# Delta rule of a hybrid decoder layer: four tiles a batch, instead of one tile at a time with the last one's scan inside

## The reference

```python
kk = jnp.einsum('nbhid,nbhjd->nbhij', kc * bc, kc)
lower = jnp.where(tri_strict, kk * decay, 0.0) + jnp.eye(c)
sol = lax.linalg.triangular_solve(lower, rhs, left_side=True, lower=True, unit_diagonal=True)
attn = jnp.einsum('nbhid,nbhjd->nbhij', qc, kc) * decay
def step(s, xs):
    u0_, wk_, attn_, qd_, kd_, gl_ = xs
    u = u0_ - jnp.einsum('bhid,bhde->bhie', wk_, s)
    o = jnp.einsum('bhid,bhde->bhie', qd_, s) + jnp.einsum('bhij,bhje->bhie', attn_, u)
    s = s * gl_[..., None, None] + jnp.einsum('bhid,bhie->bhde', kd_, u)
    return s, o
...
merged = gate[..., :D_MODEL] * (o_att @ lp['w_att_out']) + gate[..., D_MODEL:] * (o_dn @ lp['w_dn_out'])
```

## Time and profile before

| | us |
|---|---|
| median of 3 runs (lowest, highest) | 1683.84 (1683.21, 1685.87) |
| profiled execution, time | 1685.92 |
| profiled execution, span of the core | 1684.1 |
| PE busy | 1656.2 (98%) |
| weight loads busy (beside PE) | 1601.9 (95%) |
| DVE busy | 969.8 (58%) |
| ACT busy | 587.9 (35%) |
| POOL busy | 526.3 (31%) |

### The profile page before, as it was taken

The page is one execution under the profiler, slowest core; times in us unless marked ns, Lnnn a source line. Parts: engine busy times, 40 slices in busy tenths (PEclk is TensorE's granted clock), DMA queues, the critical chain, the costliest instruction groups (busy, mean ns, idle before and its releaser), DMA issues. The chain is left out here.

```text
span 1684.1 us, 34791 instructions
## 1 busy us (share of the span) xinstructions
PE 1656.2 (98%) x13952; PEld 1601.9 (95%) x13952; DVE 969.8 (58%) x1565; ACT 587.9 (35%) x1190; POOL 526.3 (31%) x287
## 2 busy tenths in 40 slices
PE   8999999999999999999999999999999999999996
PEld 7999999999999888899999999999999999999996
DVE  2001227889466677762853799877777777111157
ACT  3123334444432545542431553222322233201224
POOL 1212111111211112122431424655555554614410
PEclk9999999999999999999999999999999999999998
DMA  4111016445663455426661034444445317431202
GB/s 190 38 50 40 36 37 195 110 122 123 189 212 103 145 158 150 119 90 221 234 235 38 26 139 157 156 156 156 171 168 189 131 75 278 157 117 50 78 8 94
DMA packets 144594, 216.44 MB, mean 129 GB/s; under 512 B 66113, under 2 KB 109409, under 8 KB 142689
## 3 DMA queue, kind: packets, MB, share of 16 engines
q1 hardware_dynamic: 143488, 213.09, 37.7%
q10 hardware_dynamic: 1008, 1.98, 0.4%
HBM read 162.44 MB, written 80.00 MB: 144 GB/s over the span
## 5 line engine op out<-in xcount | busy, mean ns | idle before, releaser
L873 POOL TENSOR_TENSOR wl<-stage,wh 128x1024 fp32r<-128x1024 f32 x81 | 195.7, 2416 | 726.6 <-ACT wh L1565 718.8
L993 PE MATMUL U<-xh,wh 128*128 128x344 f32 x960 | 312.0, 325 | 0.2 <-ACT qkv L1569 0.2
L993 PE MATMUL U<-xl,wh 128*128 128x344 f32 x960 | 307.2, 320 | 0.0
L993 PE MATMUL U<-xh,wl 128*128 128x344 f32 x960 | 307.1, 320 | 0.0
L993 PEld LDWEIGHTS U<-xh,wh 128*128 128x128 f32 x960 | 181.0, 189 | 0.6 <-ACT qkv L1569 0.5
L993 PEld LDWEIGHTS U<-xh,wl 128*128 128x128 f32 x960 | 181.1, 189 | 0.0
L993 PEld LDWEIGHTS U<-xl,wh 128*128 128x128 f32 x960 | 181.0, 188 | 0.0
L1565 ACT ACTIVATE wh<-stage 128x1024 fp32r<-128x1024 f32 x77 | 81.0, 1052 | 131.2 <-PE U L993 108.0
L1104 PE MATMUL U<-xl,wh 128*128 128x344 f32 x384 | 126.3, 329 | 0.0
L1104 PE MATMUL U<-xh,wh 128*128 128x344 f32 x384 | 125.7, 327 | 0.0
L1104 PE MATMUL U<-xh,wl 128*128 128x344 f32 x384 | 125.6, 327 | 0.0
(11 more groups left out here) (456 smaller groups left out, 4441.8 us busy)
## 6 DMA issues: line engine op xcount, KB each, us to landing
stage<-in_wu SPq DMA_DIRECT2D x126, 512.0 KB, 4.3
out_shift<-in_cache SPq DMA_DIRECT2D x16, 1022.0 KB
hid_scr<-cc SPq DMA_DIRECT2D x22, 516.0 KB, 3.0
gate_scr<-gth SPq DMA_DIRECT2D x16, 516.0 KB, 3.5
gates<-gate_scr SPq DMA_DIRECT2D x8, 1032.0 KB, 5.9
dn_scr<-thb SPq DMA_DIRECT2D x12, 512.0 KB, 2.9
tok_scr<-pre SPq DMA_DIRECT2D x48, 128.0 KB, 4.0
qkv<-in_cache SPq DMA_DIRECT2D x10, 512.0 KB, 6.7
```

Of the source, the lines that this page charges most:

```text
L873: nc.gpsimd.tensor_tensor(wl[:, par, :], stage[:, par, :], wh[:, par, :].bitcast(F32), ALU.subtract).then_inc(w_lo, 1)
L993: ins = nc.tensor.matmul(dst, a[:, par, w], b[:, xk, third(j)], start=first and n == 0 and m == 0, stop=last and n == len(ks) - 1 and m == 2)
```

## The change

The tiles go in two batches of four. A batch has three phases.

1. Four fronts, each with eight quarters of gate work behind it (FRONT_FILL). Their products alternate between the banks B34 and B56. LTq, Lo32, Loff, XTq, X, Y, Lb, Xw, XT, ATm, kd, vp and dqk hold four tiles; ET, qkt, dv and Ew still hold one.
2. Six rounds of the inverse over the 16 blocks of four tiles and heads, in two halves of eight: first products of both halves, then second products of both, then the quarters of LEVEL_FILLS. ACT's and DVE's operations take a half each.
3. Four scans in a row, each with four quarters in three places (SCAN_FILLS). The transpose of the last tile's output stands inside.

To make room, oh and ol are no longer written tile by tile, as the batch's tiles lie in their place. The gated outputs (of) and the merged heads (om) go to memory, o_scr, and after the last scan six loads of 512 KB bring them back as of_raw, from which ACT and DVE form oh and ol. 74 quarters of gate work (STATE_FILLS) stand on PE behind the last scan, and 26 with the samples. The heads of the next tile are loaded when this tile's are merged.

```diff
-BESIDE_TILE = (2, 1, 1, 1, 1, 1, 1, 1, 1)
-BESIDE_SAMPLES = GATE_UNITS - EARLY - sum(BESIDE_TILE)
+BATCH = 4
+FRONT_FILL, LEVEL_FILLS, SCAN_FILLS, END_FILL = 8, (1, 1, 1, 1, 3, 2), (1, 1, 2), 2
+LATE_UNITS = GATE_UNITS - EARLY
...
+                LTq, XTq, X, Y, Lo32 = (held(zone, n, [P, BATCH * DN_H, QB]) for n in ("LTq", "XTq", "X", "Y", "Lo32"))
+                Lb = [held(zone, f"Lb{n}", [P, BATCH * DN_H, QB]) for n in range(2)]
+                Xw, Loff, Yw = (held(zone, n, [P, BATCH * DN_H, HB]) for n in ("Xw", "Loff", "Yw"))
+                XT, ATm = (held(zone, n, [P, BATCH, DN_H * P]) for n in ("XT", "ATm"))
...
+            def out_store(t):
+                sp.wait_ge(of_ready, t + 1)
+                sp.dma_start(o_scr[2:6, :, t * P:(t + 1) * P].rearrange("f p t -> p f t"), of[:, t % 2]).then_inc(out_stored.sem, 16)
...
+            for q, ts in batches():
+                for t in ts:
+                    if t + 1 < TILES:
+                        sp.wait_ge(decay_weighted, t + 1)
+                        decays(t + 1)
+                        sp.wait_ge(kd_ready, t + 1)
+                        kq_turned(t + 1)
+                        sp.wait_ge(vp_ready, t + 1)
+                        v_turned(t + 1)
+                    if t == ts[0] and t > 0:
+                        out_store(t - 1)
+                    beside.run(FRONT_FILL + (END_FILL if t == ts[0] and t > 0 else 0))
+                for n in LEVEL_FILLS:
+                    beside.run(n)
+                for t in ts:
+                    if t > ts[0]:
+                        out_store(t - 1)
+                    after(sp, of_ready, t)
+                    sp.dma_start(zin[:], dn_scr[12:16, :, t * P:(t + 1) * P].rearrange("f p t -> p f t")).then_inc(z_in, 16)
+                    if t + BATCH < TILES:
+                        sp.wait_ge(ks_done, 2 * t + 2)
+                        qk_rows(t + BATCH)
+                    sp.wait_ge(ao_ready, t + 1)
+                    sp.dma_start(o_scr[0:2, :, t * P:(t + 1) * P].rearrange("f p t -> p f t"), om[:]).then_inc(merge_stored.sem, 16)
+                    if t + 1 < TILES:
+                        heads_in(t + 1)
+                    beside.run(sum(SCAN_FILLS))
             sp.wait_ge(s_ready, TILES + 1)
             sp.dma_start(O["pS"], S[:]).then_inc(state_stored, 16)
...
+            out_store(TILES - 1)
+            sp.wait_ge(od_done, 2 * TILES)
+            sp.wait_ge(state_stored, 16)
+            since(sp, out_stored, 16 * TILES)
+            since(sp, merge_stored, 16 * TILES)
+            for k in range(6):
+                sp.dma_start(of_raw[:, k, 0:SEQ], o_scr[k]).then_inc(branch_in[k].sem, 16)
...
+            def front(t):
+                key_bank, query_bank = FRONT_BANKS[t % 2]
+                pe.wait_ge(dn_in, 16 * (t + 1))
+                if t == 0:
+                    pe.wait_ge(ao_high, 1)
+                if t % BATCH > 1:
+                    pe.wait_ge(at_ready, t - 1)
+                elif t >= BATCH:
+                    pe.wait_ge(o_ready, t - t % BATCH)
+                k, r = dqk[:, t % BATCH, 4:8, :], dqk[:, t % BATCH, 0:4, :]
+                for h, c in HEADS:
+                    nc.tensor.matmul(key_bank[:, c], k[:, h, :], k[:, h, :], start=True, stop=True)
...
+            def first_products(q, lv, a):
+                bank = FIRST_BANKS[a]
+                if lv == 0:
+                    pe.wait_ge(x_turned, 2 * q + a + 1)
+                    pe.wait_ge(at_ready, (q + 1) * BATCH)
+                else:
+                    pe.wait_ge(x_added, added_of(q, lv - 1, a))
+                if lv == LEVELS - 1:
+                    pe.wait_ge(xt_diag, 2 * q + 1)
+                for m in BLOCKS_OF[a]:
+                    if lv < LEVELS - 2:
+                        for r in QUARTER:
+                            ins = nc.tensor.matmul(bank[r, block_cols(m, QB)], Lb[(lv + 1) % 2][r, m, :], X[r, m, :],
...
+            def second_products(q, lv, a):
+                bank = SECOND_BANKS[a]
+                pe.wait_ge(y_taken, step_of(q, lv, a))
...
+            def scan(t, first):
+                q, b = t // BATCH, t % BATCH
                 pe.wait_ge(s_ready, t + 1)
+                if first:
+                    pe.wait_ge(xt_ready, turned_of(q, LEVELS - 1, 1))
                 else:
+                    pe.wait_ge(o_ready, t)
+                for h, c in HEADS:
+                    ins = nc.tensor.matmul(B34[:, 0, c], dqk[:, b, 4 + h, :], S[:, c], start=True, stop=True)
                 ins.then_inc(ks_done, 1)
+                for h, c in HEADS:
+                    ins = nc.tensor.matmul(B34[:, 1, c], dqk[:, b, h, :], S[:, c], start=True, stop=True)
+                ins.then_inc(ks_done, 1)
+                beside.run(SCAN_FILLS[0])
                 pe.wait_ge(r_ready, t + 1)
+                for h, c in HEADS:
+                    ins = nc.tensor.matmul(B34[:, 0, c], XT[:, b, c], us[:, c], start=True, stop=True)
                 ins.then_inc(u_done, 1)
+                if not first:
+                    turned(t - 1)
+                beside.run(SCAN_FILLS[1])
                 pe.wait_ge(u_taken, t + 1)
+                for h, c in HEADS:
+                    ins = nc.tensor.matmul(B34[:, 0, c], kd[:, b, h, :], us[:, c], start=True, stop=True)
+                ins.then_inc(od_done, 1)
                 pe.wait_ge(qs_taken, t + 1)
+                for h, c in HEADS:
+                    ins = nc.tensor.matmul(B34[:, 1, c], ATm[:, b, c], us[:, c], start=True, stop=True)
                 ins.then_inc(od_done, 1)
+                beside.run(SCAN_FILLS[2])
+
...
+            for q, ts in batches():
+                for t in ts:
+                    front(t)
+                    if t == ts[0] and t > 0:
+                        beside.run(END_FILL)
+                        turned(t - 1)
+                    beside.run(FRONT_FILL)
                 for lv in range(LEVELS):
+                    for a in (0, 1):
+                        first_products(q, lv, a)
+                    for a in (0, 1):
+                        second_products(q, lv, a)
+                    beside.run(LEVEL_FILLS[lv])
+                for t in ts:
+                    scan(t, t == ts[0])
+
+            beside.run(STATE_FILLS[0])
+            turned(TILES - 1)
+            beside.run(STATE_FILLS[1])
+            pe.wait_ge(of_ready, TILES)
...
+            for k in range(6):
+                beside.run(2)
+                since(act, branch_in[k], 16)
+                nc.scalar.activation(oh[:, k, 0:SEQ], of_raw[:, k, 0:SEQ], ACT.Copy).then_inc(of_high, 1)
+            nc.scalar.activation(oh[:, 0:2, SEQ:TOK], osm[:], ACT.Copy).then_inc(of_high, 1)
+            beside.run(STATE_FILLS[1] - 12 - 3)
...
+            def first_blocks(q, a):
+                pr = pair_of(a)
+                dn.link(nc.vector.tensor_tensor(XTq[:, pr], LTq[:, pr], lev(0, 8), ALU.mult))
+                nc.vector.tensor_tensor(XTq[:, pr], XTq[:, pr], fourth(D_IDQ, 8), ALU.add).then_inc(xt_ready, 1)
+                nc.vector.tensor_tensor(Lb[1][:, pr], LTq[:, pr], lev(1, 8), ALU.mult)
...
+            def heads_merged(t):
+                if t > 0:
+                    since(dve, merge_stored, 16 * t)
+                dn.link(nc.vector.tensor_tensor(ot[:, 0], ot[:, 0], ot[:, 1], ALU.add))
+                nc.vector.tensor_tensor(om[:], ot[:, 0], ot[:, 2], ALU.add).then_inc(ao_ready, 1)
...
+            for q, ts in batches():
+                for t in ts:
+                    key_norms(t)
+                    query_norms(t)
+                    if t == ts[0] and t > 0:
+                        out_scaled(t - 1)
+                    masks(t)
+                    if t == ts[0] and t > 0:
+                        out_gated(t - 1)
+                    if t + 1 < ts[0] + BATCH:
+                        decay_rows(t + 1)
+                    if t % 2 == 1:
+                        first_blocks(q, t % BATCH // 2)
+                rounds(q)
+                if ts[0] + BATCH < TILES:
+                    decay_rows(ts[0] + BATCH)
+                for t in ts:
+                    residual(t)
+                    decayed_state(t)
+                    if t > ts[0]:
+                        out_scaled(t - 1)
+                    heads_weighted(t)
+                    new_state(t)
+                    if t > ts[0]:
+                        out_gated(t - 1)
+                    out_norms(t)
+                    heads_merged(t)
+            out_scaled(TILES - 1)
+            out_gated(TILES - 1)
+            for k in range(6):
+                dve.wait_ge(of_high, k + 1)
+                nc.vector.tensor_tensor(ol[:, k, 0:SEQ], of_raw[:, k, 0:SEQ], oh[:, k, 0:SEQ].bitcast(F32), ALU.subtract).then_inc(
+                    of_low, 1)
...```

```

(22 more changed lines are left out.)

580 lines of the change are left out of this document (228 added, 352 removed).

## The result

The changed kernel takes 1764.7 us (median of four runs, 1763.9 to 1765.2) where the kernel before takes 1684.4 beside it (1683.2 to 1685.9): a ratio of 1.048, with a 95% interval of 1.046 to 1.049. It is slower by 80 us, not by the 30 that were forecast, and outside the range of 1688 to 1740.

The account below looks back on a forecast made before the run. PE's instruction stream was taken to bound the kernel (busy 98%). Shorter stream -15, waits at fronts +17.8, scans +13.6, end +10, clock +4 gave +30 us on the median, 1714 us; range 1688 to 1740.

Parts of the forecast that it names:

- I cost the rounds without a wait: Inverse rounds: copy, add and transpose of one half hide beside the other half's 0.76 us burst and the quarter.
- a batch: 25.9: PE time for a batch's six inverse rounds: 15.5 for rounds 0 to 3, 4.2 for round 4, 6.2 for round 5.
- the higher price of a record past the 32nd: Small-product bursts: if half of 2,368 records past the 32nd took twice 12 ns, 14 us more; not assumed.
- if the rounds take 6 us or more each (burst rate or clock): Sign of being wrong, in the inverse rounds: four tiles of a round were forecast at 3.9 us.
- the rounds run at 1.2 GHz: Rival: small products don't restore the clock after the wait, up to 40 us of rounds double, 1745 us; 10%.
- The fronts: Load loop 9.2 us against PE's 6.95 a front; PE waits 7.5 us before the first batch's rounds, 10.3 before the second's.
- the queue ahead of tile 1's loads: First batch's fronts: loads of tile 1 queue behind heads_in(0), 2.4 us.
- the delay of first_blocks: Fronts: first_blocks on DVE, behind the wait for ET, pushes the third tile's Ew 1.4 us further.
- The 13.6 us: Scans: heads' loop of 11.3 us against PE's 8.5 a scan costs 6.8 a batch, 13.6 in all.
- The end: After the last scan: 47.3 us of PE work, plus 10 us of waits for reloaded heads and weights, bounds 2 and 16.
- the 3 us for ACT's late evictions and splits: At the end, ACT waits for reloaded heads: PE loses 1 us, then 2 for weights that ACT splits late.
- the 4.0 put apart for the clock: Slow clock after long PE waits, about 1.5 us each at two fronts and the end, 4 us in all.

Follow-up runs that it names:

- the lump run: Changed kernel with 24 gate quarters moved from the tail into rounds 0 to 3, four together behind each round's last burst: 1754.1 us.
- spread: Changed kernel with 24 gate quarters moved from the tail into rounds 0 to 3, one behind each of a round's four bursts: 1756.8 us.
- the run with late heads: Changed kernel with DVE adding a tile's weighted heads after its new state, gated output and norms, not before the new state: 1752.3 us.
- the 33.5 us: Saving of the changed kernel with rounds 0 to 3's 32x32 products reading fp32 operands' upper halves as bf16, halving their instructions: 1731.2 us.

## Why the prediction was wrong, step by step

- **The rounds: the step that failed.** "I cost the rounds without a wait", with "a batch: 25.9". The price of a record was not the fault: as long as instructions are there, a burst of 64 at full clock takes less than the forecast's 0.76 us (128 in 1.23 with the change behind them). What was left out is the supply: 512 instructions in 7.6 us. Rounds 0 to 3 took 62.2 us instead of 31.0, so 31 us of the 48 by which the profiled span missed. Neither bound had it: the higher price of a record past the 32nd was put at 14 us at most. Its own sign of being wrong, "if the rounds take 6 us or more each (burst rate or clock)", came with 7.6 and 8.0 us, but for neither of the two reasons that it names.
- **The clock in the rounds.** Rounds 4 and 5 took 30.1 us instead of 20.8, 9 us more; at clock 1.00, in the lump run, they take 9.5, better than the 10.4 of the forecast; spread they take 11.9 at 0.86 and 17.0 at 0.59. So the clock is the cause. The rival "the rounds run at 1.2 GHz" had this mechanism at 10%, with 31 us as its price. It was right on the clock and wrong on where it counts: in rounds 0 to 3 the half clock is hidden behind the supply. The Trainium skill (TensorE: Matmul & The Clock Gate, "Part 1: The HAM clock gate") has the slow clock as the default that activity lifts; the 0.50 in the idle wait ahead of round 0 agrees, and the traces add that in the run with 12 quarters a front PE was busy for 12.70 of 12.70 us in rounds 4 and 5, and the granted clock was 0.69 on the mean.
- **The fronts.** Forecast 35.3 (four of 6.95 and 7.5 waited) and 40.0 (with 1.9 of extra work and 10.3 waited), measured 36.8 and 43.3. PE's wait ahead of round 0 was 8.0 us in the first batch (7.5 forecast) and 7.3 in the second (10.3 forecast), where PE also waited 3.8 us for ACT to evict gate work (gth), which the forecast did not have; the loop was 9.3 where 9.2 was worked out. DVE's Ew, tile by tile, as in the earlier trace rows:

```profile
530.15 0.68 DVE L2326 TENSOR_TENSOR Ew<-ET,rn 128x512 f32<-128x512 f32 x1
545.18 0.68 DVE L2326 TENSOR_TENSOR Ew<-ET,rn 128x512 f32<-128x512 f32 x1
554.49 0.69 DVE L2326 TENSOR_TENSOR Ew<-ET,rn 128x512 f32<-128x512 f32 x1
563.86 0.68 DVE L2326 TENSOR_TENSOR Ew<-ET,rn 128x512 f32<-128x512 f32 x1
```

  The first gap is 15.0 instead of 11.6, the second 9.3 instead of 10.6, the third 9.4 instead of 9.2: the queue ahead of tile 1's loads was undersized, and the delay of first_blocks, put at 1.4 for the third tile, didn't come. So part of the fit of the wait is luck. The landings were qkt 5.2 and ET 4.2 us, which the earlier trace rows had at 4.1 and 5.3.
- **The scans.** Forecast 40.3 a batch, measured 44.4 and 39.0 (the second from 747.5 to the first quarter of the tail at 786.5, which is the transpose's 793.6 less its wait of 4.6 and four quarters). DVE waited as forecast, in six scans (its list of waits; us in total, times, longest):

```profile
DVE ot L2415 <- DMA wb<-w_scr: 27.7, 6, 5.7
```

  wb landed in 5.0 us. The 13.6 us were about right: the run with late heads gives 12.4 back.
- **The end.** Forecast 47.3 and 10, measured 60.6 (786.5 to 847.1). Its waits came where they were put, ACT first for of_raw, then, as in the earlier trace rows, for the weights behind the states:

```profile
801.07 1.06 ACT L1873 ACTIVATE oh<-of_raw 128x1024 fp32r<-128x1024 f32 x1 [10.05 <-DMA of_raw<-o_scr]
...
823.85 1.06 ACT L1640 ACTIVATE wh<-stage 128x1024 fp32r<-128x1024 f32 x1 [12.48 <-DMA stage<-in_wu]
```

  and SP, as in the earlier trace rows, slower in issuing the states (7.97 us, not 2.67):

```profile
800.89 7.97 SPq L804 DMA_DIRECT2D sS<-in_sS  x4
```

  PE waited 5.2 for wl (5 forecast) and 4.6 for the last output (2 forecast); the 3 us for ACT's late evictions and splits did not come there. Together 9.8, with 10 forecast: the sum was met with parts that were not. The granted clock behind the wait was 0.90.
- **The sum.** Misses: rounds 0 to 3 +31.2, rounds 4 and 5 +9.3, fronts +1.5 and +3.3, scans +4.1 and -1.3, end +3.3, less the 4.0 put apart for the clock, and +0.8 behind 847.1 (3.3 measured, 2.5 for four owed quarters): +48.2. The span grew by 78.5, the forecast was 30. Where the clock's share lies within the +3 or so of fronts, scans and end was not taken apart.

That none of the 33.5 us came from a shorter way of a product to ACT and DVE was tested; how many instructions PE can hold ahead of itself, and why a block is not asked for sooner, was not, and stays open.

## What to carry to other kernels

Count instructions as you count time: in a run of small products PE lives on what its instruction queue brings, here a block of 256 in 3.4 to 4.0 us (some 15 ns each, two for each record, so 30 ns a record), and bursts whose records take 9 or 10 ns each are only as cheap as the long work between them lets them be. Batching small products lifts no work off the engine but takes the long work from between them; before batching, divide the batch's instructions by that rate, and put as much long work beside them as fills the difference. The list of waits shows only a part of this cost. And a loop of load, use and reload that was hidden by distance becomes a term of the time as soon as its users move together: it can be worked out from single rows beforehand, to a few us.

## What the runs showed of the hardware

- PE ran dry after 181 records of small products in a row, with as many weight loads, and then after every 128, one block of 256 instructions, in stretches with a DMA share of 0.11. The blocks start 3.4 us apart at the least though each is transferred in 0.9 to 1.5; PE's wait carries no releaser but "issue".
- The granted clock was 0.50 over 17.4 us in which PE was busy for 16.6 with 32x32 and 64x64 products and five quarters, and 1.00 before in a stretch that had the same small products between long ones. With four quarters in a lump behind each of the four rounds ahead it was 1.00 for the same 245 records, in both batches; with the four quarters spread it was 0.86 in one batch and 0.59 in the other.
- Reading fp32 operands as bf16 with a stride of two elements needed one record where fp32 needed two, and a record was shorter as well at clock 0.50: 49 in 0.56 us, against 49 of fp32 in 0.90 (first start to the last one's modelled end).
